# Routed experts of a two-layer decoder: the up projection of the next pair split around the down projection of a pair

## What is computed

```python
def moe_ffn(x, router_w, router_b, w_gate, w_up, w_down, s_gate, s_up, s_down):
    ...
    def body(y, blk):
        tok, wt, e = blk
        xb = x[tok]
        hb = jax.nn.silu(xb @ w_gate[e]) * (xb @ w_up[e])
        return y.at[tok].add((hb @ w_down[e]) * wt[:, None]), None
    ...
    shared = (jax.nn.silu(x @ s_gate) * (x @ s_up)) @ s_down
    return y + shared
```

## Time and profile before

| | |
|---|---|
| time of the runs | 1253.73 us, median of 3 (1253.66 to 1255.48) |
| span of the profiled execution | 1254.9 us |
| TensorE busy | 1201.6 us, 96% |
| VectorE, ScalarE busy | 395.3 us (32%), 296.3 us (24%) |
| read from memory | 445.75 MB, 356 GB/s over the span |
| granted TensorE clock, mean | 0.989 |
| experts of layer 0, first matmul to last combine | 193.2 to 648.7 us |

### The profile page before, as it was taken

How to read it: one execution, slowest core, us unless ns; L and a number is a source line. 1 busy time by engine, 2 the same in 40 slices (tenths; PEclk the granted TensorE clock), 3 DMA queues, 4 the chain that set the end, 5 groups by cost and what they waited for, 6 DMA issues and landing times.

```text
span 1254.9 us, 17140 instructions
## 1 busy us (share of the span) xinstructions
PE 1201.6 (96%) x6956; PEld 561.1 (45%) x6956; DVE 395.3 (32%) x892; ACT 296.3 (24%) x652; POOL 28.5 (2%) x104
## 2 busy tenths in 40 slices
PE   8998999999999999999979999999999999999995
PEld 5776754434343434434336565343434333443431
DVE  3667374212221212222143556421212111221213
ACT  3354332212121212211122343111212111221212
POOL 1005000000000000000000000000000000000000
PEclk9999999999999999999989999999999999999998
DMA  9407058999999999999993657799999999999993
GB/s 367 170 8 318 22 228 368 417 426 426 428 429 427 427 429 425 429 429 427 429 381 129 268 201 290 291 409 430 427 428 430 426 426 430 425 428 429 428 427 141
DMA packets 45024, 447.72 MB, mean 357 GB/s; under 512 B 8096, under 2 KB 9504, under 8 KB 18848
## 3 DMA queue, kind: packets, MB, share of 16 engines
q1 hardware_dynamic: 44368, 446.29, 85.0%
q10 hardware_dynamic: 592, 0.53, 0.2%
HBM read 445.75 MB, written 1.05 MB: 356 GB/s over the span
## 4 chain that ended last, share of the span: by engine, by line
PE 82%; DMA 9%; DVE 4%; ACT 2%; SPq 1%; issue 1%; DVEq 0%
PE psum L411 31%; PE psum L516 15%; DMA w_up_ring<-in_moe_up 8%; PE psum L497 4%; PE psum L427 4%; PE psum L2381 4%; PE psum L2230 4%; PE psum L1251 3%; PE psum L614 2%; PE psum L476 2%; PE psum L648 1%; PE psum L1562 1%; PE psum L1734 1%; PE psum L2387 1%; DMA w_down_ring<-in_od_w_in 1%
## 5 line engine op out<-in xcount | busy, mean ns | idle before, releaser
L411 PE MATMUL psum<-w_up_ring,moe_x_selected 128*64 128x512 f32 x2048 | 452.8, 594 | 7.5 <-DMA w_up_ring<-in_moe_up 7.4
L411 PEld LDWEIGHTS psum<-w_up_ring,moe_x_selected 128*64 128x64 f32 x2048 | 149.5, 137 | 298.6 <-issue 286.1
L516 PE MATMUL psum<-w_down_ring,moe_hT 128*64 128x512 f32 x960 | 219.3, 599 | 0.0
L1086 DVE SCALAR_TENSOR_TENSOR moe_h<-moe_silu,moe_slot_gate,psum 128x256 f32<-128x256 f32 x64 | 30.7, 480 | 392.6 <-ACT moe_silu L834 392.4
L834 ACT ACTIVATE moe_silu<-psum 128x256 f32<-128x256 f32 x64 | 24.6, 385 | 429.6 <-PE psum L411 429.6
L516 PEld LDWEIGHTS psum<-w_down_ring,moe_hT 128*64 128x64 f32 x960 | 65.2, 137 | 123.4 <-issue 107.4
L1091 DVE TENSOR_TENSOR moe_out_low<-psum,moe_out_high 128x512 fp32r<-128x512 f32 x64 | 44.2, 691 | 213.1 <-ACT moe_out_high L846 213.1
L846 ACT CAST moe_out_high<-psum 128x512 fp32r<-128x512 f32 x64 | 37.5, 586 | 129.4 <-PE psum L516 129.4
L1093 DVE TENSOR_TENSOR moe_out_low<-psum,moe_out_high 128x512 fp32r<-128x512 f32 x64 | 44.2, 691 | 63.5 <-ACT moe_out_high L848 63.5
L427 PE MATMUL psum<-moe_match,moe_x_high 128*128 128x256 f32 x224 | 60.6, 307 | 2.8 <-ACT moe_x_selected L823 2.8
L497 PE MATMUL psum<-moe_out_high,moe_matchT 32*128 32x512 f32 x496 | 62.5, 494 | 0.0
(11 more groups left out here) (543 smaller groups left out, 1064.5 us busy)
## 6 DMA issues: line engine op xcount, KB each, us to landing
w_up_ring<-in_moe_up SPq DMA_DIRECT2D x128, 2048.0 KB, 16.5
w_down_ring<-in_moe_down SPq DMA_DIRECT2D x60, 2048.0 KB, 16.3
w_up_ring<-in_ev_columns SPq DMA_DIRECT2D x4, 2048.0 KB, 16.4
w_up_ring<-in_od_w_in SPq DMA_DIRECT2D x4, 2048.0 KB, 17.6
w_up_ring<-in_ev_out SPq DMA_DIRECT2D x2, 2048.0 KB, 7.9
moe_first_down<-in_moe_down SPq DMA_DIRECT2D x2, 2048.0 KB, 9.8
w_up_ring<-in_od_w_out SPq DMA_DIRECT2D x2, 2048.0 KB, 7.8
ln_gain_bias<-in_ln_g SPq DMA_DIRECT2D x4, 512.0 KB, 7.8
```

What stands on the lines that cost most here:

```text
L411: last = nc.tensor.matmul(k.psum[e * SLOTS:(e + 1) * SLOTS, 6, :], xsel[:, kk, own:own + SLOTS], up_view(par, e, kk), start=kk == 0, stop= ...
L516: last = nc.tensor.matmul(k.psum[e * SLOTS:(e + 1) * SLOTS, bank, :], hT[:, j * P + e * SLOTS:j * P + (e + 1) * SLOTS], places[e][:, j, ha ...
```

## The change

The up projection is cut in two calls. Ahead of the turn of pair i's `h` TensorE now does the first half of pair i + 1's up projection, and the other half behind pair i's down projection. For this the up projections alternate between bank 6 (even i) and bank 5 (odd i), the gathers use banks 6, 4, 7 and come all eight together behind the last up projection of a quad, and `pe_turn_match` moves behind the down projection. At a quad's start pair 0 is not split around anything: its two halves and pair 1's first half come in a row. `shared_up(1)` now stands between the down projection of pair 13 and the second half of pair 14; the rest of the shared expert's first tile behind the first pair's second half. The overflow count is read behind the last up half. Down places are swapped, and the refills come in the new order. The core of the diff:

```diff
+    def up_bank(i):
+
+        return 6 - i % 2
...
-        def refill_up(p, i, par):
-            for half, used in enumerate((s.up_half, s.up)):
-                sp.wait_ge(used, p - 1)
-                load_up_half(sp, k, d, layer, par, 2 * i + par, half, gu[par][half])
...
+        def refill_up(p, i, half):
+            sp.wait_ge((s.up_half, s.up)[half], p - 1)
+            load_up_half(sp, k, d, layer, i % 2, p, half, gu[i % 2][half])
...
-        refill_up(2, 1, 0)
-        refill_up(3, 1, 1)
-        refill_down(5, 2, 1, 2)
-        refill_up(4, 2, 0)
-        refill_down(4, 2, 0, 3)
-        refill_up(5, 2, 1)
+        for p in (2, 3):
+            for half in range(2):
+                refill_up(p, p, half)
+        for p in (4, 5):
+            refill_up(p, p, 0)
+            refill_down(p, p, p - 2)
+            refill_up(p, p, 1)
         sp.wait_ge(s.down_b, 4)
...
+        def refill_first(q):
+            refill_up(4 * q + 2, 2, 0)
+            refill_up(4 * q + 2, 2, 1)
+            refill_up(4 * q + 3, 3, 0)
+            refill_down(4 * q + 2, 2, 4 * q + 1)
+            refill_up(4 * q + 3, 3, 1)
+
+        with sp.Fori(1, QUADS - 1) as q:
+            refill_first(q)
+            refill_up(4 * q + 4, 0, 0)
+            refill_down(4 * q + 3, 3, 4 * q + 2)
+            refill_up(4 * q + 4, 0, 1)
+            refill_up(4 * q + 5, 1, 0)
+            refill_down(4 * q + 4, 0, 4 * q + 3)
+            refill_up(4 * q + 5, 1, 1)
+            refill_down(4 * q + 5, 1, 4 * q + 4)
+        refill_first(QUADS - 1)
+        refill_down(PAIRS - 1, 3, PAIRS - 2)
...
+        def pairs_from(q, i, first=False):
+
+            for i in range(i, 3):
+                up(q, i + 1, 0)
+                turned_and_down(q, i, first=first)
+                if i == 0:
+                    pe_turn_match(6).then_inc(s.match_turned, 1)
+                if peeled(q, SHARED_UP) and i == 1:
+                    pe.wait_ge(s.shared_w, 16)
+                    shared_up(1, range(KD)).then_inc(s.shared_up, 1)
+                if peeled(q, SHARED_UP) and i == 2:
+                    shared_turn()
+                    pe.wait_ge(s.shared_wd, 16)
+                up(q, i + 1, 1)
+
+        def quad(q):
+
+            up(q, 0, 0)
+            up(q, 0, 1)
+            pairs_from(q, 0)
+            next_gathered(q)
+            turned_and_down(q, 3)
```

More of the change, by code:

```diff
@@ L395, in up_view, with pe_up @@
         return half.rearrange("p (e a k f) -> p e a k f", e=2, a=2, k=HALF)[:, e, :, kk % HALF, :]
[L398 to L402, removed]
+    def pe_up(half, par, i, bank, landed, by_tiles=False):
+        nc.tensor.wait_ge(gu[par][half], landed)
+        for kk in range(half * HALF, (half + 1) * HALF):
             if by_tiles and kk % 2 == 0:
                 nc.tensor.wait_ge((s.xsel_a, s.xsel_b)[kk // 2 % 2], 2 * (kk // 4) + 2)
[L405 to L408, removed]
             for e in range(2):
                 own = (2 * i + e) * SLOTS
-                last = nc.tensor.matmul(k.psum[e * SLOTS:(e + 1) * SLOTS, 6, :], xsel[:, kk, own:own + SLOTS],
+                last = nc.tensor.matmul(k.psum[e * SLOTS:(e + 1) * SLOTS, bank, :], xsel[:, kk, own:own + SLOTS],
                                         up_view(par, e, kk), start=kk == 0, stop=kk == KD - 1)
-            if kk == HALF - 1:
-                last.then_inc(s.up_half, 1)
         return last
@@ L649, in shared_down @@
                                  start=False, stop=True, skip_group_check=True)
[L651 to L664, removed]
         def shared_turn():
@@ L694, in pair @@
             pe.wait_ge(s.matchT, q + 1 if i else q)
[L695 to L700, removed]
             if first and i == 1:
@@ L703, in pair @@
             pe_combine((i - 1) % 4, 0, begin=first and i == 1).then_inc(s.half_combined, 1)
[L704 to L709, removed]
             pe.wait_ge(s.h, p + 1)
-            pe_turn().then_inc(s.turned, 1)
+            pe_turn(up_bank(i)).then_inc(s.turned, 1)
             pe.wait_ge(s.half_combined, p)
@@ new lines, in quad, with first_quad @@
+        def quad(q):
[4 more added lines that the diff above has]
+            turned_and_down(q, 3)
+        def first_quad():
+            pe_up(0, 0, 0, 6, 16, by_tiles=True).then_inc(s.up_half, 1)
+            pe_up(1, 0, 0, 6, 16, by_tiles=True).then_inc(s.up, 1)
+            pe.wait_ge(s.quad_gates, 1)
+            pe.wait_ge(s.match_bf, 1)
+            pe_slot_gates().then_inc(s.slot_gates, 1)
+            up(0, 1, 0)
+            pe.wait_ge(s.h, 1)
+            pe_turn(6).then_inc(s.turned, 1)
+            pe.wait_ge(s.turned_sb, 1)
+            pe.wait_ge(x.dn_first, 16)
+            pe_down([first_down[:, 0], first_down[:, 1]], 0, 4).then_inc(s.down_a, 1)
+            pe_down([first_down[:, 0], first_down[:, 1]], 1, 7).then_inc(s.down_b, 1)
+            pe_turn_match(6).then_inc(s.match_turned, 1)
+            up(0, 1, 1)
+            shared_up(0, range(5, KD)).then_inc(s.shared_up, 1)
+            pairs_from(0, 1, first=True)
+            next_gathered(0)
+            turned_and_down(0, 3, first=True)
@@ L731, in tensor @@
+        first_quad()
         with pe.Fori(1, SHARED_UP) as q:
-            for i in range(4):
-                pair(q, i)
+            quad(q)
         for q in (SHARED_UP, SHARED_DOWN):
-            for i in range(4):
-                pair(q, i)
+            quad(q)
         with pe.Fori(SHARED_DOWN + 1, QUADS - 1) as q:
[L738 to L741, removed]
+            quad(q)
+        up(QUADS - 1, 0, 0)
```

135 lines of the change are left out of this document (70 added, 65 removed).

## The result

The changed kernel takes 1263.82 us (median of 4 runs, 1260.54 to 1265.79); the kernel before 1254.10 in the same comparison. The ratio is 1.0071, with a 95% interval of 1.006 to 1.0083: slower by 7.5 to 10.4 us. I had put it at 1257.1, with 1260.5 as the upper end: the direction was right, the loss nearly three times as large as forecast (9.7 us by the medians, 3.4 forecast).

What follows compares the result with a forecast made beforehand. The weights' queue was taken as the bound. A layer: -1.3 + 1.2 + 1.6 + 0.4 = +1.9 us; both layers less 0.4 give +3.4, from 1253.7 to 1257.1 us, range 1251.5 to 1260.5.

Steps and rivals of the forecast that it cites:

- What bounds the kernel now: Experts of a layer: the full weights' queue sets the end, 58.9 us a quad against TensorE's 54 to 55.
- The places of the waits: TensorE waits for weights at pair 14 half 0, 2.6 us, and pair 30 half 0, 4 to 5.5 us.
- 20.9 us of work against 19.7 of transfers: Last quad, pair 30 half 0 to pair 31 half 1: TensorE's work exceeds four transfers by 1.2 us.
- The last half lands 1.3 us earlier: Weights' queue: holes of 3.0 us instead of 4.3 bring the last up half 1.3 us earlier; ends 0 and 4.3.
- The hole at the start: Weights' queue, empty from 208.5 to 212.8 us, 4.3 us; smaller holes, together 3.0 us, were to replace it.
- The loss behind pair 14's wait costs nothing; it shortens the next wait: Clock loss after pair 14 half 0's wait: no cost, as it only shortens the wait at pair 30 half 0.
- Clock loss, 1.6 us: Behind pair 30 half 0's wait TensorE runs at half clock: 1.6 us a layer, ends 0 and 3.5.
- Read of the overflow count, 0.4 us: End of a layer's experts: pair 31's combine and turn queue behind this read, partly covered, 0.4 us a layer.
- Between the layers, -0.4 us: TensorE's 0.77 us wait for `kv_w` between the layers shrinks if TensorE is late: -0.4 us.
- The rivals: Whole kernel: no loss of clock, 1253 to 1255.5 us, 0.25; faster by queue or TensorE, 0.13; slower still, 0.14.
- slower still: Cold stretch twice as long, or queue empty at quad starts too: 1259 to 1263 us, chance 0.14.

Runs made afterwards that it cites:

- e2: The changed kernel with 5 extra matmuls filling the wait ahead of pair 30 half 0, output the same: 1258.88 us.
- e6: As e2, with the 5 extra matmuls ahead of pair 14 half 0 as well, in each layer: 1256.39 us.
- e3: The changed kernel, from the third quad on, with pair 4q+2's up half 0 refilled ahead of pair 4q+1's down weights: 1254.34 us.
- e12: The changed kernel with e3's refills up to the last quad and e5's last quad: 1254.89 us.
- e7: The changed kernel with half the bytes in each weight refill, output differs: 1275.89 us, total unusable (overflow pass in layer 1); layer 0's experts 444.3 us.
- e8: The kernel before with half the bytes in each weight refill, output differs: 1245.68 us; layer 0's experts 450.9 us.
- e10: The kernel before, unedited, run once more for a second trace: 1254.17 us.
- e11: The changed kernel, unedited, run once more for a second trace: 1263.65 us.
- e1: The changed kernel with the last quad's up projections done whole, behind the down projection of the pair before, refills as changed: 1265.18 us.
- e5: As e1, with the last quad's refills in the order of its work, pair 30's down weights ahead of pair 31's halves: 1256.72 us.

## Why the prediction fell short

The medians split the 9.7 us: 4.9 go with e2 (clock at pair 30), 2.5 more with e6 (clock at pair 14), and e6 still lies 2.4 above the kernel before beside it. That rest fits the longer work behind pair 30 half 0: from there to pair 31 half 1 it is 20.9 us in e6 and 19.5 in the kernel before, 1.4 us a layer. In short, the refills bring pair 30 half 0 and pair 14 half 0 later than the new order of the work wants them. By the steps of the prediction:

- **"What bounds the kernel now"**: right. e3 and e12 end where the kernel before ends, although the new order has 6.7 us a layer less for TensorE (e7, e8). I had counted 3.3; about 4 us are the waits ahead of the turns (for `h`) and of the gathers (for ScalarE) that are gone. Where the rest comes from isn't settled.
- **The places of the waits**: right. Pair 14 half 0 and pair 30 half 0, none between there and the last half. At pair 30 it came to 5.2 us (4 to 5.5 forecast), at pair 14 to 5.2 (2.6 forecast). The second is longer above all because the weights came later than forecast. Counted from the first up matmul, TensorE asked for pair 14 half 0 at 182.7 us (379.39 - 5.18 - 191.47) where I had 183.2 (376.4 - 193.25), and could start at 187.9 where I had 185.8 (379.0 - 193.25).
- **20.9 us of work against 19.7 of transfers**: right, 20.9 in e2 and e6.
- **"The last half lands 1.3 us earlier"**: the step that failed most. Counted from the first up matmul, pair 30 half 0 started at 423.7 us before (616.94 - 193.25) and 423.9 in e10, but at 424.3 and 425.1 after. With layer 1 (425.1 and 423.8 before, 425.3 and 425.4 after) the means are 424.1 and 425.0: 0.9 us later, with a scatter of more than 1 us within one kernel. In e6 the mean is 424.2. So of the 2.2 us between forecast and measurement 0.7 go with pair 14's cold matmuls, the next point; the other 1.4 or so are the gain that never came. The hole at the start shrank little: over the first 70 us of the experts the queue loses 4.8 and 4.5 us in the two traces of the changed kernel, 5.0 and 5.2 in those of before (sum of (427 - rate) / 427 over windows of 10 us). I had summed only the times in which nothing moves; the rows at 325 to 378 GB/s above show that over stretches of 6 us the queue also stays below its rate. The refills are issued singly there, some us apart; that this is the reason is my reading, and no run tests it. The gain was lost before any long wait: pair 14 half 0, issued at 358.31 us, landed 20.9 us later, 187.7 us behind the first up matmul, and before at 187.1 (361.64 + 18.7 - 193.25). Only then comes the second hole, 1.6 and 2.1 us, 290 us in.
- **"The loss behind pair 14's wait costs nothing; it shortens the next wait"**: wrong. It delays the places that TensorE frees behind it, and 290 us in the queue runs dry (e6); that it does so there because the shared expert has used up TensorE's lead is argued, not tested. I asked who waits for TensorE there, and not for whom TensorE frees places. Together with the step above this is the larger part of the miss: 2.2 of some 3.1 us a layer.
- **Clock loss, 1.6 us**: the mechanism was right, the size too small. 6.63 - 3.65 = 3.0 us in layer 0, 2.5 in layer 1, 1.7 and 1.5 in e11; 2.5 us a layer by the medians of e2. I had one case for it, 1.9 us, and took a part off for the wait's own cover, which no row had shown. The Trainium skill, TensorE: Matmul & The Clock Gate, section "HAM oscillation — how this bites in real kernels", says that a burst after a wait for transfers starts cold. The trace agrees, with 0.50 from 615.6 to 621.6 us; e2 shows 1.00 with the same wait filled.
- **Read of the overflow count, 0.4 us**: 0. From the start of pair 31 half 1 to its down projection it is 5.68 us before (642.10 - 636.42) and 5.63 after, so the 16 matmuls sent ahead cover it.
- **Between the layers, -0.4 us**: 0. From pair 31 half 1 to the first matmuls of the next mixer it is 19.50 before and 19.44 after. The wait of 0.77 us is still there, and the trace now names ScalarE's copy as its releaser, not the transfer.
- **The rivals**: "slower still" came true, by both of its mechanisms, and the time lies just above its 1259 to 1263 us: the cold stretch was dearer, and the queue ran dry once more, 290 us in. I gave it 0.14 and counted its two mechanisms as alternatives; here both follow from the long waits and add up.

## What to carry to other kernels

Here a queue of transfers ends the stage, and the time that the new order saves TensorE was worth nothing, even with matching refills (e3, e12). With refills in another order than the work wants them it was a loss: a transfer moved past another, once a layer or once a quad, is worth 8.5 and 9.5 us (e1 against e5, the change against e3). A delay that looks hidden because a wait follows must also be asked for what it frees: the price of pair 14's cold matmuls came out 100 us later, in the queue. And short scattered waits can be cheaper than their sum in one piece, since the long one also takes the clock down.

## What was not expected of the hardware

- Behind waits of nearly equal length (5.06 to 5.19 us, the eight at pairs 14 and 30 in the two traces of the changed kernel) the same 16 matmuls took between 5.06 and 6.63 us, and 3.65 without a wait: the clock's cost of one such wait is 1.4 to 3.0 us, and a single case does not fix it. After waits of 1.2 us (e3) they took 3.65.
- Five matmuls whose result is overwritten, 4.56 us of otherwise idle time in each layer, held the clock at 1.00 and made the kernel 4.9 us faster (e2).
- The first up matmul of layer 0 starts between 190.1 and 194.0 us in the traces (190.14 in e2, 194.04 in e6), of kernels that are the same up to there. Single spans can mislead by that much. The stretch from that matmul to pair 31 half 1 repeats better, but not exactly: over two traces and both layers it takes 443.2 to 444.6 us before and 447.7 to 448.7 in the changed kernel.
